# State space matrices turned inside a feed-forward layer's last step, and the mixer's closing units in split products

## The chip, the cores and the metric

The kernel runs on one core of a Trainium2 chip. The metric is device time in microseconds (us) for one execution of the whole program. TensorE is called PE in the profile, VectorE DVE, ScalarE ACT, GpSimd POOL and SyncE SP. "PEld" is PE's loading of weights, which overlaps with its matmuls.

## What is computed

256 tokens of width 1024 pass through two layers of a first block (a hybrid mixer, then a dense SwiGLU or eight experts) and two layers of a second block (SwiGLU, a mixer, SwiGLU). Two places matter here. The first is the end of the hybrid mixer, which runs once in each layer of the first block:

```
y_dn = o.reshape(B, S, DN_V) @ w_up_dn           # 1024 x 1024
y_sb = o_sb.reshape(B, S, SB_W) @ w_up_sb        #  512 x 1024
g_dn, g_sb = jnp.split(jax.nn.sigmoid(gates), N_BRANCH, axis=-1)
return (g_dn * y_dn + g_sb * y_sb) @ w_out       # 1024 x 1024
```

The second is the start of the second block's first mixer, a state space recurrence, which follows the third feed-forward layer (`ffn1_0`) of the program:

```
h = h + 0.5 * _swiglu(_rmsnorm(h, ffn1_norm[layer]), ffn1_w_in[layer], ffn1_w_out[layer])
u = _rmsnorm(h, mix_norm[layer])
bu_re = jnp.einsum('bsgh,gph->bsgp', ug, bb_re)  # ug: u in groups of 16 channels
bu_im = jnp.einsum('bsgh,gph->bsgp', ug, bb_im)
_, _, x_re, x_im = lax.associative_scan(combine, (la_re, la_im, bu_re, bu_im), axis=1)
```

## The kernel before

**Layout and order.** Activations lie with channels on the 128 partitions: 8 channel tiles of 256 tokens side by side. Each engine has its own list of instructions, written out by hand, and the lists meet only at semaphores; an instruction that waits holds up all that is behind it on its engine. Weights come in *units* of 128x2048 numbers (1 MB) through a ring of six buffers: SP loads unit n when unit n-6 is done (`unit_done` counts finished units). One unit holds 16 blocks of 128x128 and is multiplied with 256 tokens.

**Two ways to multiply a unit.** `cols_unit` (L419 to L431) multiplies plain f32 weights from the ring with f32 activations, 16 matmuls. `cols_split` (L488 to L497) takes weights and activations as two fp32r parts each, high and low, and makes three matmuls for each block (`product`, L483 to L486: high by high, high by low, low by high). For that, ACT copies a unit's high part to one of two places, `room[n % 2]` (`w_hi`, L2187 to L2191), and DVE subtracts it from the ring's unit, which gives the low part in `ring_low` (`w_low`, L1261 to L1266; its instruction has line L1234, as every `tt` of DVE has). `w_hi` of unit n waits until the units up to n-2 are done. The activations are split the same way in quarters of 128x512, counted by `h_high` and `h_low`. All feed-forward layers and the mixer's first projection use `cols_split`; `SPLITS` numbers the units in the order in which they are split, and `INPUTS` the split activations.

**The mixer's end** (`combine`, L709 to L732) has ten units, all in f32: `up` 0 to 3 (delta rule output by `w_up_dn`), `up` 4 and 5 (attention output by `w_up_sb`), `w_out` 0 to 3. Between `up` 0 and `up` 1 stands `stick` (L697), 16 small products of the attention, in banks 2 and 3 of PSUM; DVE copies these banks out (L1774, L1775, `stick_out`), and `up` 2 waits for that. DVE multiplies each `up` result with its gates as it comes, adds the two branches (`mixed`, by quarters), and adds the `w_out` results to the residual `X` (L1790). Unit `w_out` 0 is written out by itself (L728) since it takes the quarters of `mixed` as they come. Then come the sum of squares of the norm (`norm`, PE, L441), its logarithm and exponential (ACT, L2237 and L2238), and the normalising (DVE, L1253).

**The start of the recurrence.** The last unit of `ffn1_0` is the last step of `ffn_split` (L891): its results lie in banks 4 to 7, finished two tiles at a time (`bank_out`), and DVE adds each to `X` (L1875). Then PE sums squares for norm 6, DVE normalises (eight instructions, L1253), and only when all eight are done does PE turn the 16 blocks of the recurrence's input matrices (`BBX`, L1013), which DVE copies out of banks 0, 1, 4 and 5 (L1955) to `BBT`. After that PE makes the first products of channel block k = 0 (L1048) into banks 0 to 3, and DVE begins its loop over k: two multiplies out of PSUM, two sums, two scans (L1982, L1983), two multiplies. `BBX` itself was made by DVE beside the units of `ffn1_0`.

Of the kernel before, what the change touches and what calls it, by code (L numbers as in the profile page):

```python
# [22 lines left out]
P = 128  # L23
# [55 lines left out]
MIXER = dict(mixer_v=("a_abs", "gu", "cum_read", "kd_arg", "u_arg", "q_dec", "vnew0", "state", "vt_out", "vnew1", "stick_out"),  # L79
# [6 lines left out]
def program(nc, A):  # L86
    ctx = ExitStack()
    with ctx:
# [148 lines left out]

        def w_high(room, n):
            return room[n % 2]
# [4 lines left out]
        ROOM = ROOM_MIX = (SLOT["E"], SLOT["D"], SLOT["F"])  # L244
        ROOM_GLU = (11264, 13312, 23552)
# [3 lines left out]
        NORM_BANK = (7, 7, 0, 7, 7, 7, 0, 4, 0, None, 0, 7)  # L249
# [5 lines left out]
        for name, count in (("w_in0", 0), ("ffn", BLK1), ("w_in1", 0), ("ffn1_0", BLK2), ("ffn2_0", BLK2), ("ffn1_1", BLK2),  # L255
                            ("ffn2_1", BLK2)):
            SPLITS[name], SPLIT_BLOCKS[name] = splits, blocks_before
            splits += 3 * count if count else PROJECTIONS
            blocks_before += count
# [151 lines left out]
        def _(pe):  # L411
# [21 lines left out]
            def half(b, t):  # L433
                return bank[b][:, t * TOK:(t + 1) * TOK]

# [52 lines left out]
            def cols_split(n, dst, room, first=None):  # L488

                for t in range(2):  # L490
                    for k in range(KT):
                        if first is not None and t == 0 and k % 2 == 0:
                            pe.wait_ge(*at("h_low", k // 2 + 1, INPUTS[first]))
                        c = (k * 2 + t) * P
                        mm = product(dst(t), parts(w_high(room, n) + c, P), ring_low[n % RING][:, c:c + P],
                                     parts(h_high(room) + k * TOK, TOK), parts(HB + k * TOK, TOK), k == 0, k == KT - 1)
                mm.then_inc(sem("unit_done"), 1)  # L497
# [211 lines left out]
            def combine(l):  # L709
                n = UN[f"up{l}"]  # L710
                pe.wait_ge(*at("stick_arg", 2, l, 8))
                for u in range(4):
                    if u == 1:
                        stick(l)
                    if u == 2:
                        pe.wait_ge(*mixer("stick_out", l))
                    cols_unit(n + u, lambda t: half(u, t), src=BIG, src_off=OD,
                              quarter=None if u else lambda b: at("od", b, l, 4))
                for u in range(2):
                    cols_unit(n + 4 + u, lambda t: half(4 + 2 * u + t // 2, t % 2), kt=4, tiles=4, src=BIG, src_off=OSB)  # L720
# [10 lines left out]
                for u in range(1, 4):  # L731
                    cols_unit(n + u, lambda t: half(u, t), src=BIG, src_off=SLOT["D"])  # L732
# [158 lines left out]
            def ffn_split(name, blocks, base, room):  # L891
# [3 lines left out]
                def step(p, i=0):  # L895
# [13 lines left out]
                    else:  # L909
# [11 lines left out]
                        if p == 3 * blocks - 1:  # L921
                            if name == "ffn":
                                ada_later(MIX_UNITS, 12, bank[1], 0)

# [82 lines left out]
            norm(6, 0)  # L1007

            pe.wait_ge(*at("normed", 8, 6))
            pe.wait_ge(sem("bb"), 1)  # L1010
            for i in range(2):
                for k in range(KT):
                    mm = pe.transpose(bank[4 * i + k // 4][:, (k % 4) * P:(k % 4 + 1) * P], big(BBX + i * 1024 + k * P, P), ident)  # L1013
            mm.then_inc(sem("bt_ps"), 1)
# [26 lines left out]
            for k in range(KT + 2):  # L1041
                if k < KT:

                    if k:
                        pe.wait_ge(sem("bu_read"), k)
# [183 lines left out]
        def _(ve):  # L1229
# [356 lines left out]
            for l in range(LAYERS):  # L1586
# [186 lines left out]
                ve.wait_ge(*mixer("stick_ps", l))  # L1773
                ve.tensor_copy(big(OSB, 512), bank[2][:, :])  # L1774
                ve.tensor_copy(big(OSB + 512, 512), bank[3][:, :]).then_inc(mixer("stick_out", l)[0], 1)  # L1775

                n = UN[f"up{l}"]
                for b in range(4):
                    ve.wait_ge(sem("unit_done"), n + b + 1)
                    tt(big(SLOT["D"] + b * 512, 512), bank[b][:, :], big(GATES + b * 512, 512), ALU.mult)  # L1780
                for b in range(4):
                    if b % 2 == 0:
# [3 lines left out]
                        .then_inc(sem("mixed"), 1)  # L1786
                n = UN[f"w_out{l}"]
                for t in range(KT):
                    ve.wait_ge(sem("unit_done"), n + t // 2 + 1)
# [161 lines left out]
            norm_v(norms, ("mix_norm", 0), False)  # L1951
            norms += 1
            ve.wait_ge(sem("bt_ps"), 1)
            for b in range(4):
                ins = ve.tensor_copy(big(BBT + b * 512, 512), bank[(0, 1, 4, 5)[b]][:, :])  # L1955
# [3 lines left out]
            lk(ve.memset(view(SM, MAG, [[TOK, 4], [1, 1]]), 0.0))  # L1959
            for k in range(KT):  # L1960
# [220 lines left out]
        def _(se):  # L2181
# [5 lines left out]
            def w_hi(n, room, i=0):  # L2187

                se.wait_ge(sem(f"loaded{n % RING}"), i * 16 + 16 * (n // RING + 1))
                se.wait_ge(sem("unit_done"), i * RING + (n - 1))  # L2190
                act(parts(w_high(room, n), UNIT), ring[n % RING][:, :], ACT.Copy).then_inc(sem("w_high"), 1)  # L2191
# [163 lines left out]
            for l in range(LAYERS):  # L2355
# [484 lines left out]
```

## Time and profile before

| | us |
|---|---|
| median of 3 timed runs | 3281.03 |
| lowest, highest | 3277.46, 3284.76 |
| the profiled execution, device time | 3277.59 |
| its span in the trace | 3275.8 |
| granted PE clock, mean over the span | 0.971 |

Some 1.8 us of the profiled execution's time lie outside the span. All starts and durations below are of that one execution, in us from the start of its span. "The chain" is the chain of work that ended last, followed back from the last instruction; "issue" in it is time in which the engine waited for nothing that the profile shows.

### The profile page before, as it was taken

The page shows a single profiled execution, that of the slowest core. Times are in us where ns is not written, and L with a number is a line of the kernel's source. Part 1 is how long each engine was busy: PE and PEld are TensorE (multiplying, and loading weights), DVE is VectorE, ACT ScalarE, POOL GpSimd, SP SyncE. Part 2 cuts the span into 40 slices and gives each one's busy share as a digit, 9 for nine tenths or more (in the row PEclk, how much of TensorE's full clock was granted, in tenths as well). Part 3 has the DMA queues.
Part 4 walks back from the last instruction along what each step waited for, and adds up shares of the span by engine and source line. Part 5 has one row for each costly group of instructions (what it writes and reads, how often), then busy time and mean ns, then how long its engine had stood idle before and what let it go on. Part 6 is the DMA issues. An engine that isn't in the chain of part 4 may idle for free.

```text
span 3275.8 us, 48712 instructions
## 1 busy us (share of the span) xinstructions
PE 3129.9 (96%) x20334; PEld 2804.2 (86%) x20334; DVE 2290.1 (70%) x2552; ACT 1632.4 (50%) x1637; POOL 111.4 (3%) x118
## 2 busy tenths in 40 slices
PE   7999999999999999999999999899589999998999
PEld 7999899999898788888888888899259999995799
DVE  7975288838662888988988988597974435447344
ACT  3546144435461777777777777343114324435333
POOL 0004000000120000000000000000000000100000
PEclk8999999989999999999999999999689999998999
DMA  8640388735303699999999999354023543540253
GB/s 360 250 150 1 116 309 307 264 114 187 116 1 129 217 368 366 367 369 366 371 364 368 361 375 365 132 187 171 1 102 143 186 172 142 193 166 14 103 181 128
DMA packets 130019, 702.96 MB, mean 215 GB/s; under 512 B 11184, under 2 KB 15552, under 8 KB 74048
## 3 DMA queue, kind: packets, MB, share of 16 engines
q1 hardware_dynamic: 118816, 650.30, 53.8%
q0 software_dynamic: 6880, 48.24, 3.8%
q10 hardware_dynamic: 4160, 2.12, 0.3%
q8 instruction: 118, 1.93, 0.2%
q14 instruction: 45, 0.37, 0.0%
HBM read 698.50 MB, written 1.07 MB: 214 GB/s over the span
## 4 chain that ended last, share of the span: by engine, by line
PE 90%; DVE 6%; ACT 2%; issue 1%; POOL 1%; DMA 0%; SPq 0%; ACTq 0%; DVEq 0%
PE banks L484 23%; PE banks L485 23%; PE banks L486 23%; PE banks L428 7%; DVE big L1234 2%; PE banks L592 1%; PE banks L441 1%; PE banks L574 1%; PE banks L786 1%; DVE ring_low L1234 1%; PE banks L1063 1%; PE banks L480 1%; PE banks L580 1%; POOL tail L2628 1%; PE banks L807 1%
## 5 line engine op out<-in xcount | busy, mean ns | idle before, releaser
L1234 DVE TENSOR_TENSOR ring_low<-ring,parts 128x2048 fp32r<-128x2048 f32 x570 | 1297.6, 2287 | 375.9 <-ACT parts L2191 351.1
L484 PE MATMUL banks<-parts 128*128 128x256 f32 (+1 forms) x3712 | 1168.0, 315 | 20.9 <-DVE tail_parts L1234 17.5
L485 PE MATMUL banks<-tail_parts,parts 128*128 128x256 f32 x3744 | 1062.5, 284 | 0.0
L2191 ACT ACTIVATE parts<-ring 128x2048 fp32r<-128x2048 f32 x234 | 448.5, 1917 | 808.4 <-PE banks L486 708.6
L486 PE MATMUL banks<-parts,ring_low 128*128 128x256 f32 x2816 | 798.1, 283 | 0.0
L484 PEld LDWEIGHTS banks<-parts 128*128 128x128 f32 x3712 | 706.7, 190 | 61.8 <-issue 20.2
L2264 ACT ACTIVATE parts<-ring 128x2048 fp32r<-128x2048 f32 x336 | 644.8, 1919 | 211.7 <-DMA ring<-in_wall 207.9
L485 PEld LDWEIGHTS banks<-tail_parts,parts 128*128 128x128 f32 x3744 | 712.8, 190 | 1.9 <-issue 1.9
L486 PEld LDWEIGHTS banks<-parts,ring_low 128*128 128x128 f32 x2816 | 537.8, 191 | 0.0
L486 PE MATMUL banks<-parts,tail_parts 128*128 128x512 f32 x896 | 352.6, 394 | 0.0
L485 PE MATMUL banks<-ring_low,parts 128*128 128x512 f32 x896 | 352.5, 393 | 0.0
L484 PE MATMUL banks<-tail_parts,parts 128*128 128x256 f32 x928 | 263.0, 283 | 0.1
L486 PE MATMUL banks<-tail_parts,ring_low 128*128 128x256 f32 x928 | 262.6, 283 | 0.0
L486 PEld LDWEIGHTS banks<-parts,tail_parts 128*128 128x128 f32 x896 | 168.3, 188 | 40.7
L485 PEld LDWEIGHTS banks<-ring_low,parts 128*128 128x128 f32 x896 | 168.8, 188 | 33.9
L484 PE MATMUL banks<-parts,tail_parts 128*128 128x512 f32 x448 | 177.5, 396 | 1.0 <-DVE tail_parts L1234 1.0
L484 PEld LDWEIGHTS banks<-tail_parts,parts 128*128 128x128 f32 x928 | 177.1, 191 | 0.4 <-issue 0.4
L486 PEld LDWEIGHTS banks<-tail_parts,ring_low 128*128 128x128 f32 x928 | 176.8, 191 | 0.0
L485 PE MATMUL banks<-ring_low,tail_parts 128*128 128x512 f32 x448 | 176.3, 394 | 0.0
L486 PE MATMUL banks<-parts 128*128 128x512 f32 x448 | 176.3, 393 | 0.0
L428 PE MATMUL banks<-big,ring 128*128 128x256 f32 x768 | 167.4, 379 | 0.8 <-DVE big L2173 0.8
L428 PEld LDWEIGHTS banks<-big,ring 128*128 128x128 f32 x768 | 145.5, 190 | 21.2 <-DVE big L2173 1.2
(408 smaller groups left out, 3397.6 us busy)
## 6 DMA issues: line engine op xcount, KB each, us to landing
ring<-in_wall SPq DMA_DIRECT2D x616, 1024.0 KB, 6.5
big<-in_wall POOLq DMA_DIRECT2D x40, 1024.0 KB, 5.7
big<-in_w_k POOLq DMA_DIRECT2D x1, 2048.0 KB, 9.4
big<-in_w_v POOLq DMA_DIRECT2D x1, 2048.0 KB, 16.5
big<-bias_table ACTq DMA_DIRECT2D x2, 1024.0 KB, 7.8
constants<-in_con SPq DMA_DIRECT2D x1, 1249.5 KB, 9.4
x<-in_x SPq DMA_DIRECT2D x1, 1024.0 KB, 7.1
big<-big POOLq DMA_DIRECT2D x16, 64.0 KB, 5.1
```

What stands on the lines that cost most here:

```text
L428: mm = pe.matmul(dst(t), tile(n, k * tiles + t), src[:, src_off + k * width:src_off + (k + 1) * width], start=(k == 0), stop=(k == kt - 1))
L441: mm = pe.matmul(half(b, 0), ones, big(SQ0 + t * TOK, TOK), start=(t == 0), stop=(t == KT - 1))
L480: mm = pe.matmul(o[:, c:c + 1], ada_sum(first + n)[:, t * P:(t + 1) * P], ones[:, 0:1], start=True, stop=True)
L484: pe.matmul(o, high, in_high, start=start, stop=False, **kw)
L485: pe.matmul(o, high, in_low, start=False, stop=False, **kw)
L486: return pe.matmul(o, low, in_high, start=False, stop=stop, **kw)
L574: mm = pe.matmul(bank[q][:, c * P:(c + 1) * P], block(LTS, q, c), block(SLOT["E"], q, c), start=True, stop=True)
L580: mm = pe.transpose(bank[4 + q % 2][:, c * P:(c + 1) * P], block(SLOT["E"], q, c), ident)
L592: mm = pe.matmul(bank[6 + q % 2][:, c * P:(c + 1) * P], inverse_t, u, start=True, stop=True)
L1234: return ve.tensor_tensor(out, a, b, op)
L2191: act(parts(w_high(room, n), UNIT), ring[n % RING][:, :], ACT.Copy).then_inc(sem("w_high"), 1)
L2264: act(parts(slot_at(q), UNIT), ring[r][:, :], ACT.Copy).then_inc(sem("x_high"), 1)
```

## The change

In the mixer's end, `up` 1 to 5 and `w_out` 1 to 3 become split products; `up` 0 and `w_out` 0 stay in f32. ACT and DVE get the splitting of these eight weight units a layer and of three inputs (`OD`, the attention output, `mixed`), at the places in their lists that the diff shows. The copying of banks 2 and 3 by DVE becomes four half-bank copies by ACT and four subtractions by DVE. At the recurrence, the turning moves into the last step of `ffn1_0`, before its products; DVE copies the turned blocks right after its last addition to `X`; the norm's sum goes to bank 4; and PE's first products wait for their own channel block of the normalised input.

```diff
+        ROOM_UP, ROOM_OUT, SUM_LOW, OSB_HIGH = (0, CONV, SLOT["C"]), (0, CONV + 2048, SLOT["C"]), SLOT["B"], OSB + 1024
-        NORM_BANK = (7, 7, 0, 7, 7, 7, 0, 4, 0, None, 0, 7)
+        NORM_BANK = (7, 7, 0, 7, 7, 7, 4, 4, 0, None, 0, 7)
...
             def combine(l):
                 n = UN[f"up{l}"]
                 pe.wait_ge(*at("stick_arg", 2, l, 8))
-                for u in range(4):
-                    if u == 1:
-                        stick(l)
+                cols_unit(n, lambda t: half(0, t), src=BIG, src_off=OD, quarter=lambda b: at("od", b, l, 4))
+                stick(l)
+                for u in range(1, 4):
                     if u == 2:
-                        pe.wait_ge(*mixer("stick_out", l))
-                    cols_unit(n + u, lambda t: half(u, t), src=BIG, src_off=OD,
-                              quarter=None if u else lambda b: at("od", b, l, 4))
+                        pe.wait_ge(*at("h_low", 4, INPUTS[f"osb{l}"]))
+                    pe.wait_ge(sem("w_low"), SPLITS[f"od{l}"] + u)
+                    cols_split(n + u, lambda t: half(u, t), ROOM_UP, f"od{l}" if u == 1 else None, SUM_LOW)
                 for u in range(2):
-                    cols_unit(n + 4 + u, lambda t: half(4 + 2 * u + t // 2, t % 2), kt=4, tiles=4, src=BIG, src_off=OSB)
+                    pe.wait_ge(sem("w_low"), SPLITS[f"od{l}"] + 4 + u)
+                    for t in range(4):
+                        for k in range(4):
+                            c = (k * 4 + t) * P
+                            mm = product(half(4 + 2 * u + t // 2, t % 2), parts(w_high(ROOM_UP, n + 4 + u) + c, P),
+                                         ring_low[(n + 4 + u) % RING][:, c:c + P], parts(OSB_HIGH + k * TOK, TOK),
+                                         parts(OSB + k * TOK, TOK), k == 0, k == 3)
+                    mm.then_inc(sem("unit_done"), 1)
...
                 for u in range(1, 4):
-                    cols_unit(n + u, lambda t: half(u, t), src=BIG, src_off=SLOT["D"])
+                    pe.wait_ge(sem("w_low"), SPLITS[f"mixed{l}"] + u)
+                    cols_split(n + u, lambda t: half(u, t), ROOM_OUT, f"mixed{l}" if u == 1 else None, SUM_LOW)
```

PE, the last step of `ffn_split`, and then the start of the recurrence:

```diff
+                            if name == "ffn1_0":
+                                pe.wait_ge(sem("bb"), 1)
+                                for c in range(2 * KT):
+                                    turned_b = pe.transpose(bank[c // 4][:, (c % 4) * P:(c % 4 + 1) * P], big(BBX + c * P, P), ident)
+                                turned_b.then_inc(sem("bt_ps"), 1)
...
-            norm(6, 0)
-
-            pe.wait_ge(*at("normed", 8, 6))
-            pe.wait_ge(sem("bb"), 1)
-            for i in range(2):
-                for k in range(KT):
-                    mm = pe.transpose(bank[4 * i + k // 4][:, (k % 4) * P:(k % 4 + 1) * P], big(BBX + i * 1024 + k * P, P), ident)
-            mm.then_inc(sem("bt_ps"), 1)
+            norm(6, 4)
             pe.wait_ge(sem("bt"), 1)
...
+                    pe.wait_ge(*at("normed", k + 1, 6))
```

DVE, the mixer's end, behind the attention's arguments:

```diff
-                ve.wait_ge(*mixer("stick_ps", l))
-                ve.tensor_copy(big(OSB, 512), bank[2][:, :])
-                ve.tensor_copy(big(OSB + 512, 512), bank[3][:, :]).then_inc(mixer("stick_out", l)[0], 1)
+                def sum_low(name, source):
+                    for b in range(4):
+                        ve.wait_ge(*at("h_high", b + 1, INPUTS[name]))
+                        tt(parts(SUM_LOW + b * 512, 512), big(source + b * 512, 512),
+                           parts(h_high(ROOM_UP) + b * 512, 512).bitcast(F32), ALU.subtract).then_inc(sem("h_low"), 1)
...
+                sum_low(f"od{l}", OD)
+                w_low(n + 1, SPLITS[f"od{l}"] + 1, ROOM_UP)
+                for c in range(4):
+                    ve.wait_ge(*at("h_high", c // 2 * 2 + 2, INPUTS[f"osb{l}"]))
+                    tt(parts(OSB + c * TOK, TOK), half(2 + c // 2, c % 2), parts(OSB_HIGH + c * TOK, TOK).bitcast(F32), ALU.subtract)                        .then_inc(sem("h_low"), 1)
+                w_low(n + 2, SPLITS[f"od{l}"] + 2, ROOM_UP)
                 for b in range(4):
                     ve.wait_ge(sem("unit_done"), n + b + 1)
                     tt(big(SLOT["D"] + b * 512, 512), bank[b][:, :], big(GATES + b * 512, 512), ALU.mult)
+                    if b:
+                        w_low(n + 2 + b, SPLITS[f"od{l}"] + 2 + b, ROOM_UP)
+                w_low(n + 7, SPLITS[f"mixed{l}"] + 1, ROOM_OUT)
...
+                sum_low(f"mixed{l}", SLOT["D"])
                 n = UN[f"w_out{l}"]
                 for t in range(KT):
+                    if t in (0, 2):
+                        w_low(n + 2 + t // 2, SPLITS[f"mixed{l}"] + 2 + t // 2, ROOM_OUT)
```

DVE, the start of the recurrence:

```diff
             ffn2("ffn1_0", 0)
+            ve.wait_ge(sem("bt_ps"), 1)
+            for b in range(4):
+                ins = ve.tensor_copy(big(BBT + b * 512, 512), bank[b][:, :])
+            lk(ins)
+            ve.nop().then_inc(sem("bt"), 1)
+
+            lk(ve.memset(view(SM, MAG, [[TOK, 4], [1, 1]]), 0.0))
             norm_v(norms, ("mix_norm", 0), False)
             norms += 1
-            ve.wait_ge(sem("bt_ps"), 1)
-            for b in range(4):
-                ins = ve.tensor_copy(big(BBT + b * 512, 512), bank[(0, 1, 4, 5)[b]][:, :])
-            lk(ins)
-            ve.nop().then_inc(sem("bt"), 1)
-
-            lk(ve.memset(view(SM, MAG, [[TOK, 4], [1, 1]]), 0.0))
```

ACT, the mixer's end, behind the attention's exponentials (`w_hi` gets an argument `done`, 1 where nothing is said, and waits for `unit_done` to reach `n - done`):

```diff
+                def sum_high(b, source):
+                    act(parts(h_high(ROOM_UP) + b * 512, 512), big(source + b * 512, 512), ACT.Copy).then_inc(sem("h_high"), 1)
+                n = UN[f"up{l}"]
+                for b in range(4):
+                    se.wait_ge(*at("od", b + 1, l, 4))
+                    sum_high(b, OD)
+                w_hi(n + 1, ROOM_UP)
+                w_hi(n + 2, ROOM_UP)
+                se.wait_ge(*mixer("stick_ps", l))
+                for c in range(4):
+                    act(parts(OSB_HIGH + c * TOK, TOK), half(2 + c // 2, c % 2), ACT.Copy).then_inc(sem("h_high"), 1)
+                for u in range(3, 6):
+                    w_hi(n + u, ROOM_UP)
+                w_hi(n + 7, ROOM_OUT, done=2)
+                for b in range(4):
+                    se.wait_ge(*at("mixed", b + 1, l, 4))
+                    sum_high(b, SLOT["D"])
+                w_hi(n + 8, ROOM_OUT)
+                w_hi(n + 9, ROOM_OUT)
```

## Rows read from the trace of the kernel before

**Rows 1.** The page: busy time by engine, and the chain by engine.

```profile
PE 3129.9 (96%) x20334; PEld 2804.2 (86%) x20334; DVE 2290.1 (70%) x2552; ACT 1632.4 (50%) x1637; POOL 111.4 (3%) x118
PE 90%; DVE 6%; ACT 2%; issue 1%; POOL 1%; DMA 0%; SPq 0%; ACTq 0%; DVEq 0%
```

**Rows 2.** The chain at both mixers' ends: start us, us, what.

```profile
349.77 34.73 PE banks L428 x160
384.50 6.91 PE banks L728 x32
391.41 20.72 PE banks L428 x96
412.13 3.47 PE banks L441 x16
991.41 34.73 PE banks L428 x160
1033.05 20.72 PE banks L428 x96
```

**Rows 3.** Windows: one split unit, then five f32 units (clock and DMA share behind).

```profile
2276.43:2282.15 5.72, 5.72 (x49) 5.72 (x49) 2.08 (x3) 1.90 (x3) 0.00 (x0) 1.00 0.52 186
349.77:384.50 34.73, 34.73 (x162) 30.60 (x162) 6.63 (x10) 0.00 (x0) 0.00 (x0) 1.00 0.40 140
```

**Rows 4.** Timelines of ACT and DVE: splitting of a weight unit, of a quarter.

```profile
427.76 1.91 ACT L2191 ACTIVATE parts<-ring 128x2048 fp32r<-128x2048 f32 x1 [4.71 <-PE banks L486]
422.41 0.63 ACT L2250 ACTIVATE parts<-tail 128x512 fp32r<-128x512 f32 x1
429.70 2.29 DVE L1234 TENSOR_TENSOR ring_low<-ring,parts 128x2048 fp32r<-128x2048 f32 x1 [3.74 <-ACT parts L2191]
420.16 0.69 DVE L1234 TENSOR_TENSOR tail_parts<-tail,parts 128x512 fp32r<-128x512 f32 x1
```

**Rows 5.** Timelines of ACT, DVE and PE around the first f32 unit and stick.

```profile
340.44 1.77 ACT L2473 ACTIVATE big<-big 128x768 f32<-128x768 f32 x2 [1.03 <-DVE big L1234]
339.39 1.94 DVE L1234 TENSOR_TENSOR big<-big,banks 128x384 f32<-128x384 f32 x4
346.90 0.66 PE L704 MATMUL banks<-big,tail 128*64 128x256 f32 x4
2327.71 0.38 ACT L2511 ACTIVATE big<-banks 128x256 f32<-128x256 f32 x1 [0.17 <-PE banks L1063]
```

**Rows 6.** Timeline of DVE: gates and branch sums.

```profile
377.63 0.69 DVE L1234 TENSOR_TENSOR big<-banks,big 128x512 f32<-128x512 f32 x1 [6.21 <-PE banks L428]
378.97 0.68 DVE L1234 TENSOR_TENSOR big<-banks,big 128x512 f32<-128x512 f32 x1
```

**Rows 7.** The chain at the start of the recurrence.

```profile
2282.15 3.47 PE banks L441 x16
2286.60 3.26 DVE tail L1253 x8
2289.91 3.00 PE banks L1013 x16
2292.93 2.49 DVE big L1955 x4
2295.53 2.13 PE banks L1048 x16
2297.75 4.50 DVE big L1234 x2
```

**Rows 8.** Timeline of PE: four transposes, and what follows, in the delta rule.

```profile
260.55 0.60 PE L580 MATMUL banks<-constants,big 128*128 128x128 f32 x4
260.99 1.06 PE L574 MATMUL banks<-big,tail 128*128 128x128 f32 x8
```

**Rows 9.** Timeline of DVE: its last addition to X before norm 6.

```profile
2282.19 0.69 DVE L1875 SCALAR_TENSOR_TENSOR x<-banks,x 128x512 f32<-128x512 f32 x1 [0.74 <-PE banks L486]
```

**Rows 10.** Windows of 4 us in and behind the recurrence: granted clock third from the end.

```profile
2288.00:2292.00 4.00, 2.09 (x13) 2.10 (x14) 1.85 (x5) 0.00 (x0) 0.00 (x0) 0.83 0.00 0
2420.00:2424.00 4.00, 4.00 (x23) 4.00 (x22) 3.97 (x3) 0.00 (x0) 0.00 (x0) 0.55 0.02 4
```

More of the change, by code:

```diff
@@ L78 @@
 SUMMED = (0, 1, 2, 3, 4, 5, 6, 7, 8, 10, 11)
-MIXER = dict(mixer_v=("a_abs", "gu", "cum_read", "kd_arg", "u_arg", "q_dec", "vnew0", "state", "vt_out", "vnew1", "stick_out"),
+MIXER = dict(mixer_v=("a_abs", "gu", "cum_read", "kd_arg", "u_arg", "q_dec", "vnew0", "state", "vt_out", "vnew1", ),
              mixer_s=("beta_exp", "a_ln", "decay_exp", "u_exp", "w_neg"),
@@ L232, in parts, with half @@
             return PARTS[:, off:off + width]
+        def half(b, t):
+            return bank[b][:, t * TOK:(t + 1) * TOK]
         def w_high(room, n):
@@ L254, in program @@
         splits = blocks_before = 0
-        for name, count in (("w_in0", 0), ("ffn", BLK1), ("w_in1", 0), ("ffn1_0", BLK2), ("ffn2_0", BLK2), ("ffn1_1", BLK2),
-                            ("ffn2_1", BLK2)):
+        for name, count, blocks in (("w_in0", PROJECTIONS, 0), ("od0", 5, 0), ("osb0", 0, 0), ("mixed0", 3, 0), ("ffn", 3 * BLK1, BLK1),
+                                    ("w_in1", PROJECTIONS, 0), ("od1", 5, 0), ("osb1", 0, 0), ("mixed1", 3, 0),
+                                    ("ffn1_0", 3 * BLK2, BLK2), ("ffn2_0", 3 * BLK2, BLK2), ("ffn1_1", 3 * BLK2, BLK2),
+                                    ("ffn2_1", 3 * BLK2, BLK2)):
             SPLITS[name], SPLIT_BLOCKS[name] = splits, blocks_before
-            splits += 3 * count if count else PROJECTIONS
-            blocks_before += count
+            splits += count
+            blocks_before += blocks
         INPUTS = {name: i for i, name in enumerate(SPLITS)}
@@ L431, in cols_unit @@
                 mm.then_inc(sem("unit_done"), 1)
-            def half(b, t):
-                return bank[b][:, t * TOK:(t + 1) * TOK]
             def norm(i, b):
@@ L486, in product, with cols_split @@
                 return pe.matmul(o, low, in_high, start=False, stop=stop, **kw)
-            def cols_split(n, dst, room, first=None):
+            def cols_split(n, dst, room, first=None, low=HB):
                 for t in range(2):
@@ L495, in cols_split @@
                         mm = product(dst(t), parts(w_high(room, n) + c, P), ring_low[n % RING][:, c:c + P],
-                                     parts(h_high(room) + k * TOK, TOK), parts(HB + k * TOK, TOK), k == 0, k == KT - 1)
+                                     parts(h_high(room) + k * TOK, TOK), parts(low + k * TOK, TOK), k == 0, k == KT - 1)
                 mm.then_inc(sem("unit_done"), 1)
@@ L1950, in _ @@
             ffn2("ffn1_0", 0)
-            norm_v(norms, ("mix_norm", 0), False)
-            norms += 1
             ve.wait_ge(sem("bt_ps"), 1)
             for b in range(4):
-                ins = ve.tensor_copy(big(BBT + b * 512, 512), bank[(0, 1, 4, 5)[b]][:, :])
+                ins = ve.tensor_copy(big(BBT + b * 512, 512), bank[b][:, :])
             lk(ins)
@@ L1959, in _ @@
             lk(ve.memset(view(SM, MAG, [[TOK, 4], [1, 1]]), 0.0))
+            norm_v(norms, ("mix_norm", 0), False)
+            norms += 1
             for k in range(KT):
@@ L2185, in lk, with w_hi @@
                 link(se, "scalar_step", ins)
-            def w_hi(n, room, i=0):
+            def w_hi(n, room, i=0, done=1):
                 se.wait_ge(sem(f"loaded{n % RING}"), i * 16 + 16 * (n // RING + 1))
-                se.wait_ge(sem("unit_done"), i * RING + (n - 1))
+                se.wait_ge(sem("unit_done"), i * RING + (n - done))
                 act(parts(w_high(room, n), UNIT), ring[n % RING][:, :], ACT.Copy).then_inc(sem("w_high"), 1)
```

## The prediction

> **What bounds the kernel now.** I read the page's busy times and its chain first, then the chain in order of time around the two places that change, then the timelines of ACT and DVE there, and last the windows for the granted clock. The page says that PE is busy 96% of the span and carries 90% of the chain, DVE 6% [rows 1]. So time is won where PE's own work shrinks, or where PE and DVE hand the chain to each other for nothing. Both places show one of these. At the mixer's end the chain is PE alone, without a gap: `up` 1 to 5 run in 34.73 us, `w_out` 0 in 6.91, `w_out` 1 to 3 in 20.72, and norm 1 follows at 412.13; layer 1 repeats it [rows 2]. An f32 unit thus costs 6.91 us at the full clock (the window says 1.00) [rows 3]. In those 34.73 us DVE works 6.63 us and ACT not at all [rows 3]: there is room for splitting. At the recurrence the chain changes hands six times: norm sum, normalising by DVE, turning by PE, copies by DVE, the first products by PE, and DVE's loop from 2297.75 on [rows 7].
>
> **The mixer's end, PE.** A split unit in the feed-forward layer before norm 6 takes 5.72 us at clock 1.00, with its 48 matmuls of 128x256 and without idle time [rows 3]. That row is for the same matmul shapes that the eight units of a layer get. `up` 4 and 5 have another order (4 tiles by 4 blocks) but the same 16 blocks. So `up` 1 to 5 go from 34.73 to 28.60 (6.13 less), `w_out` 1 to 3 from 20.72 to 17.16 (3.56 less): 9.69 us a layer if PE never waits.
>
> The Trainium skill, FP8 and Floating Point Precision, section TensorE Precision Notes, says that a true FP32 product takes four passes through the array. Three products in place of four passes would make a unit 5.18 us (three quarters of 6.91), and the gain 13.8 us a layer in place of 9.69. The row of the split unit disagrees: 5.72, and the sum goes by the row.
>
> **Does the splitting keep up?** One weight unit costs ACT 1.91 us, then DVE 2.29; a quarter of activations 0.63 and 0.69 [rows 4]. I walk through layer 0.
>
> *Start.* ACT's exponentials end at 342.2 and DVE's arguments at 341.3 [rows 5]. ACT copies four quarters (about 0.54 apiece back to back) to 344.4 and unit `up` 1 to 346.3; DVE follows with its quarters to 345.1 and the unit from 346.3 to 348.6. `stick` begins at 346.90 [rows 5] and gives way to `up` 1 at 349.77 [rows 2]. So `up` 1 starts on time, with 1.1 us to spare; `up` 0 and `stick` are the work that hides this. Without them the 1.91 + 2.29 us would stand in the open.
>
> *Attention output.* ACT's copy for `up` 2 waits for `up` 0 (about 347.0) and ends at 348.9. Behind it stand the four half-bank copies, which start when `stick` is done; 0.38 us for 256 columns out of PSUM [rows 5], about 0.3 apiece in a run, so to 351.1. DVE subtracts to 351.8 and only then makes the low part of `up` 2, to 354.1. `up` 1 ends at 349.8 + 5.7 = 355.5: 1.4 us to spare. The two DVE copies that this replaces lay in the same place, beside `up` 1.
>
> *Steady state.* A unit's high part can start when the unit two before it is done, so the pair has one unit's duration, 5.72 us. It needs 1.91 + 2.29 and a hop between engines, 4.3 us. DVE's gate multiply of 0.69 [rows 6] falls in the 1.91 of ACT. That leaves 1.4 us at each of `up` 3 to 5. By this walk `up` 4 ends at 372.7 and `up` 5 at 378.4.
>
> *Into `w_out`.* Here the order in DVE's list costs something. The low part of `w_out` 1 stands ahead of the sums with the second branch. ACT starts its high part when `up` 4 is done (`done=2`), 372.7 to 374.6; DVE makes the low part until 376.9. Only then come the first two pairs of gate multiply and sum, 1.34 us a pair [rows 6], so `mixed` 1 at 378.3, `mixed` 2 at 379.7, 3 at 381.0 and 4 at 382.4. `w_out` 0 starts at 378.4, uses the first quarter for 0.86 us (4 of 32 instructions of 6.91 us) and stands 0.4 us for the second; the others are there before their turn, since both tiles of the first half come first. I take 0.5 us. In the kernel before, the first two quarters were long there when `up` 5 ended. `w_out` 0 ends at about 385.8. What is late next: ACT's quarters of `mixed` at 383.1, DVE's at 384.9, so `w_out` 1 has 0.9 us to spare. `w_out` 2 and 3 are split as in the steady state (each DVE part before two X updates of 0.88 together, which wait for units long done). PE then ends about 9.2 us earlier than 412.13. The norm behind it is as before, for it hangs on the last X update; ACT's list is empty there.
>
> Bounds of this part: 9.69 a layer with no stall. The other end is a stall as long as the smallest margin lets through: if each of seven hand-overs (all but the first) took 1.9 us longer than I sum, 0.5 us of it would show at each, 3.5 us a layer. I take 9.2, twice 18.4.
>
> SP's loads are triggered by `unit_done` and come at 5.7 in place of 6.9 us: the DMA share was 0.40 there and 0.52 in a stretch at the new pace [rows 3], so they stay hidden. POOL's loads wait for the X updates, as before.
>
> **The recurrence.** Before, DVE's loop starts 2297.75 - 2282.15 = 15.60 us after the last product of `ffn1_0` [rows 7]. Removed from that stretch are the turning (3.00), the copies (2.49), and the first products (2.13), with their hops [rows 7]. The first products of k = 0 now need only the first of DVE's eight normalising instructions: PE starts 0.5 us after 2286.60 and needs 2.13, so it ends at 2289.2, under DVE's 3.26, which end at 2289.86 [rows 7]. DVE then goes straight on at 2289.90, 7.85 us earlier. The copies need cover: the last addition to X ends at 2282.88 [rows 9], four copies end at 2285.4, the two links and the memset at about 2285.8, and the reciprocal root that DVE waits for comes at 2286.60: 0.8 us to spare. Without it, 2.49 would be back. ACT's first scalar row waits for the copies too, and is wanted only by the scan, some 7 us into the loop.
>
> Added is the turning in front of the last step's products. PE has no idle time there (5.72 busy of 5.72) [rows 3], so it costs all it lasts. 16 transposes cost 3.00 us where they were, but the clock was 0.83 and falling there [rows 7, 10]. At full clock four of them pass in 0.44 us (260.55 to 260.99) [rows 8], so sixteen in 1.76. `ffn1_0` runs at clock 1.00, so I take 1.76; 3.00 is the other end. Their four banks were read before the wait on the last `g_low`, which PE does anyway. Gain: 7.85 - 1.76 = 6.1 us (4.8 at the other end). It is kept: everything behind starts from DVE's loop.
>
> **The sum.** 18.4 + 6.1 = 24.5 us. Against the profiled execution's own 3277.59 (1.8 outside the span) that is 3253.1. The runs' median lies 3.4 above it, which gives 3256.5. I take 3255, between the two. 0.2%, what a measurement of this kernel can tell from no change, is 6.6 us.
>
> **Rivals.**
> 1. *Late feed.* The hand-overs cost more than I sum and 0.5 us shows at seven places a layer: 3255 + 7 = 3262. For it: three engines in turn, margins of 0.9 to 1.4 us. Against: the feed-forward layers feed their units by the same two instructions and run without idle time [rows 3]. Chance 0.08.
> 2. *The feed sets the pace at about the old one*, 6.9 us a unit: nothing is won at the mixer. It needs 2.6 us more in each round than the rows give. Then only the 6.1 us of the recurrence stay: 3273, no measurable change. Chance 0.04.
> 3. *The feed is serial, and the kernel slower.* Place: the room of a unit's high part. If it came free only when the unit just before is done, each of the 16 units would cost 5.72 + 1.91 + 2.29 = 9.92 in place of 6.91, 48 us in all less the 6.1: 3321. A serial unit costs 3.0 and a good one gives 1.2, so with the recurrence's gain it decides from about six serial units of the sixteen. Against it: two rooms alternate, as in the feed-forward layers. Chance 0.03.
> 4. *The recurrence gives 2 us or less*, because the copies delay the normalising, or because the PE waits inside DVE's loop grow by what was won at its start: 3259. Chance 0.04.
> 5. *A split block costs three quarters of an f32 one.* PE would need 5.18 us a unit, 8.6 us less than my sum over 16 units: 3246. [...] The trace does not agree (5.72). Chance 0.03.
>
> My forecast has the remaining 0.78. Its own spread comes from the clock. It drops when PE pauses, and even in a busy stretch (0.55 at 2420) [rows 10]. A shifted program meets these drops at other points, each worth a microsecond or two, and the timed runs spread over 7.3 us. Rivals 1 and 4 lie inside 3246 to 3264, rival 5 at its lower edge, 2 and 3 outside. Faster: 0.78 + 0.08 + 0.04 + 0.03 = 0.93; same 0.04; slower 0.03.
>
> **What the changed profile would show.** The eight units a layer take 28.6 and 17.2 us in the chain, lines 484 to 486 in place of 428. PE idles about 0.4 us within `w_out` 0, released by DVE, and nowhere else in the mixer's end. The turning takes 1.8 us before the last step of `ffn1_0`. DVE's first loop multiply follows the eight normalising instructions at once. I would be wrong if PE idles before `up` 1 or at each split unit with DVE as the releaser, if the 16 transposes take 3 us, or if DVE's normalising waits for its own copies.

## The result

The changed kernel takes 3257.91 us (median of 4 runs, 3253.88 to 3259.99), the kernel before 3279.53 us in the runs timed with it (4 runs, 3277.46 to 3284.76). The ratio is 0.993 with a 95% interval of 0.9913 to 0.9947: 21.6 us less by the medians, 17.4 to 28.5 by the interval. The forecast was 3255.0, inside 3246 to 3264, and "faster by over 0.2%" (6.6 us). The profiled execution took 3257.01 us with a span of 3255.2, 20.6 less than the span of before.

The chain of the changed kernel at the mixer's end of layer 0, in order of time (L434 is `cols_unit`, L738 is `w_out` 0, L444 the norm sum, L2218 and L1244 are ACT's and DVE's splitting):

```profile
340.23 6.91 PE banks L434 x32
373.11 1.93 ACT parts L2218
375.06 2.29 DVE ring_low L1244
377.98 1.30 DVE big L1244 x2
380.06 6.31 PE banks L738 x28
403.51 3.47 PE banks L444 x16
```

These answer to [rows 2], and to one more row of the chain before, the start of its `up` 0:

```profile
340.06 6.91 PE banks L428 x32
```

From the start of `up` 0 to the norm sum it is now 63.28 us; before it was 72.07 (412.13 less 340.06). The split matmuls between these rows are too short and too many to be listed. The window over the whole stretch, DVE's list where the chain leaves PE, and PE's list at the same place:

```profile
340.23:403.51 63.28, 63.05 (x482) 60.16 (x481) 36.14 (x41) 27.61 (x27) 0.00 (x0) 1.00 0.42 150
```

```profile
369.34 2.29 DVE L1244 TENSOR_TENSOR ring_low<-ring,parts 128x2048 fp32r<-128x2048 f32 x1 [1.31 <-ACT parts L2218]
375.06 2.29 DVE L1244 TENSOR_TENSOR ring_low<-ring,parts 128x2048 fp32r<-128x2048 f32 x1 [3.42 <-ACT parts L2218]
377.27 0.68 DVE L1244 TENSOR_TENSOR big<-banks,big 128x512 f32<-128x512 f32 x1
377.98 0.69 DVE L1244 TENSOR_TENSOR big<-big 128x512 f32<-128x512 f32 x1
378.59 0.68 DVE L1244 TENSOR_TENSOR big<-banks,big 128x512 f32<-128x512 f32 x1
379.31 0.69 DVE L1244 TENSOR_TENSOR big<-big 128x512 f32<-128x512 f32 x1
```

```profile
378.44 0.28 PE L489 MATMUL banks<-parts,ring_low 128*128 128x256 f32 x1
378.82 7.54 PE L738 MATMUL banks<-big,ring 128*128 128x256 f32 x32
```

PE is busy 63.05 of 63.28 us at clock 1.00, and DVE's low parts start 5.72 us apart (369.34 and 375.06), the pace of the split unit: the feed keeps up. DVE waits 3.42 us for ACT before it makes the low part of `w_out` 1 (375.06), and its gate multiplies stand behind that. The first sum is ready at 378.67, the second at 380.00. The last product of `up` 5 starts at 378.44 and such products follow each other every 0.12 us (48 in 5.72), so the first sum comes 0.1 us too late, and `w_out` 0 starts at 378.82. It then has the matmuls of one quarter before it needs the second sum: the chain comes back to L738 with 28 of 32 instructions left, at 380.06, and the unit's 32 matmuls take 7.54 us from first start to last end.

The chain at the recurrence, which answers to [rows 7] (L938 is the turning, L1263 the normalising, L1244 DVE's first loop multiplies):

```profile
2263.26 1.75 PE banks L938 x16
2270.72 3.47 PE banks L444 x16
2275.25 3.26 DVE tail L1263 x8
2278.50 4.41 DVE big L1244 x2
```

The turning costs 1.75 us in the last step of `ffn1_0`, and DVE's loop follows the normalising without a gap, 7.78 us after the last product in place of 15.60. The copies lie in DVE's list directly behind its last addition, and DVE still waits 1.15 us for ACT's root after them:

```profile
2271.37 2.47 DVE L1980 COPY big<-banks 128x512 f32<-128x512 f32 x4
2274.03 0.06 DVE L1984 MEMSET small<- 128x4 f32 x1 [0.19 <-DVE big L1980]
2275.25 3.26 DVE L1263 SCALAR_TENSOR_TENSOR tail<-x,parameters,inverse_rms 128x256 f32<-128x256 f32 x8 [1.15 <-ACT inverse_rms L2265]
```

**Where 3 us went.** The stretches that the change touches are shorter by 8.79, 8.78 and 7.82 us, and `ffn1_0` pays 1.75. That makes 23.64, not 20.6. The chains show where time came back: from norm 1 to norm 2, code that the diff leaves alone, it was 259.72 us before and is now 262.21; from norm 3 to the gathering of tokens 17.61 and now 19.25. These two make 4.1 us; all the other stretches that the change leaves alone together are 1.1 us shorter (behind the glu units 2.4 less, DVE's loop 1.0 more). Windows from the first feed-forward product to norm 2 and from norm 3 to the gathering, with PE's busy time and matmul records and the granted clock third from the end, first before, then changed:

```profile
419.53:671.85 252.32, 251.71 (x2065) 0.98 0.75 283
1053.77:1071.38 17.61, 12.90 (x71) 0.81 0.16 61
```

```profile
410.91:665.72 254.81, 254.46 (x2065) 0.97 0.74 281
1038.89:1058.14 19.25, 14.54 (x70) 0.73 0.17 55
```

The extra time is PE's busy time, 2.75 and 1.64 us more for the same matmuls at a lower granted clock, and no longer wait. Windows of 2 us at the start of the first feed-forward layer show the difference (the granted clock stands third from the end). First the kernel before, then the changed one:

```profile
419.00:421.00 2.00, 1.19 (x7) 0.92 (x7) 2.00 (x5) 1.94 (x6) 0.00 (x0) 0.79 0.96 389
421.00:423.00 2.00, 2.00 (x9) 1.89 (x10) 1.31 (x3) 1.97 (x4) 0.00 (x0) 0.50 1.04 434
423.00:425.00 2.00, 2.00 (x14) 1.85 (x14) 1.92 (x2) 0.04 (x1) 0.00 (x0) 0.85 1.00 422
```

```profile
409.00:411.00 2.00, 0.09 (x1) 0.12 (x1) 1.55 (x4) 1.94 (x5) 0.00 (x0) 0.80 0.97 365
411.00:413.00 2.00, 2.00 (x9) 1.96 (x10) 2.00 (x6) 1.97 (x5) 0.00 (x0) 0.50 1.02 426
413.00:415.00 2.00, 2.00 (x11) 1.90 (x9) 1.23 (x3) 1.40 (x3) 0.00 (x0) 0.50 1.01 426
415.00:417.00 2.00, 2.00 (x10) 1.90 (x10) 2.00 (x2) 0.00 (x0) 0.00 (x0) 0.50 1.02 430
417.00:419.00 2.00, 2.00 (x19) 2.00 (x18) 0.35 (x1) 0.00 (x0) 0.00 (x0) 1.00 0.73 307
```

In both, PE idles some 4 us for the norm, the clock falls to 1.2 GHz (0.50) at about the time when PE starts again, and the first products run at that level. Before, it was back at 2.4 GHz after some 3.5 us; now it stays low for about 7. The experiments had to say whether the change does that. (The clock fell ahead of norm 2 as well, in both: it was 0.50 from 664 to 668 before and from 656 to 660 now.)

### The profile page after: what moved, and what is told of

Same layout as the page of the kernel before. It is cut to its first block, busy times and chain, and to the rows that moved or that the text cites. A ratio compares the mean times of both kernels' runs of the same rounds, so it can differ in the third digit from the quotient of the medians.

```text
span 3255.2 us, 49327 instructions
## 1 busy us (share of the span) xinstructions
PE 3113.2 (96%) x20590; PEld 2801.0 (86%) x20590; DVE 2335.6 (72%) x2588; ACT 1675.0 (51%) x1677; POOL 111.3 (3%) x118
## 4 chain that ended last, share of the span: by engine, by line
PE 89%; DVE 7%; ACT 2%; issue 1%; POOL 1%; DMA 1%; SPq 0%; ACTq 0%; DVEq 0%
PE banks L487 24%; PE banks L488 23%; PE banks L489 23%; PE banks L434 4%; DVE big L1244 2%; PE banks L595 1%; PE banks L444 1%; PE banks L577 1%; DVE ring_low L1244 1%; PE banks L797 1%; PE banks L483 1%; PE banks L583 1%; POOL tail L2677 1%; DVE tail L1244 1%; DMA ring<-in_wall 1%
## 5 line engine op out<-in xcount | busy, mean ns | idle before, releaser
L1244 DVE TENSOR_TENSOR ring_low<-ring,parts 128x2048 fp32r<-128x2048 f32 x586 | 1334.3, 2287 | 411.5 <-ACT parts L2218 379.7
L487 PE MATMUL banks<-parts 128*128 128x256 f32 (+1 forms) x3968 | 1240.3, 313 | 21.5 <-DVE tail_parts L1244 18.1
L2218 ACT ACTIVATE parts<-ring 128x2048 fp32r<-128x2048 f32 x250 | 479.2, 1917 | 797.7 <-PE banks L489 752.7
L489 PE MATMUL banks<-parts,ring_low 128*128 128x256 f32 x3072 | 869.8, 283 | 0.0
L487 PEld LDWEIGHTS banks<-parts 128*128 128x128 f32 x3968 | 754.7, 190 | 63.3 <-issue 20.5
L2291 ACT ACTIVATE parts<-ring 128x2048 fp32r<-128x2048 f32 x336 | 644.9, 1920 | 208.1 <-DMA ring<-in_wall 202.2
L489 PEld LDWEIGHTS banks<-parts,ring_low 128*128 128x128 f32 x3072 | 585.8, 191 | 0.0
L1244 DVE TENSOR_TENSOR big<-big 128x512 f32<-128x512 f32 (+6 forms) x141 | 124.8, 891 | 29.1 <-ACT big L2575 20.1
L1244 DVE TENSOR_TENSOR tail<-tail,banks 128x256 f32<-128x256 f32 (+1 forms) x170 | 86.0, 506 | 55.0 <-PE banks L489 49.1
```

What stands on the lines that cost most here:

```text
L487: pe.matmul(o, high, in_high, start=start, stop=False, **kw)
L489: return pe.matmul(o, low, in_high, start=False, stop=stop, **kw)
L1244: return ve.tensor_tensor(out, a, b, op)
L2291: act(parts(slot_at(q), UNIT), ring[r][:, :], ACT.Copy).then_inc(sem("x_high"), 1)
```

## The experiments

Stretches are read off each kernel's chain, in us of its one profiled execution; all kernels are listed together behind the experiments. Times of kernels with one run say nothing to 0.1%, so the stretches carry those verdicts.

### Each part alone, and both kernels once more

`mixer_only` is the changed kernel with the recurrence as before, `turn_only` the kernel before with the recurrence as changed:

```diff
 # mixer_only, against the changed kernel (PE; the turning in ffn1_0 and the waits per block are gone, DVE has the old order too)
-            norm(6, 4)
+            norm(6, 0)
+
+            pe.wait_ge(*at("normed", 8, 6))
+            pe.wait_ge(sem("bb"), 1)
+            for i in range(2):
+                for k in range(KT):
+                    mm = pe.transpose(bank[4 * i + k // 4][:, (k % 4) * P:(k % 4 + 1) * P], big(BBX + i * 1024 + k * P, P), ident)
+            mm.then_inc(sem("bt_ps"), 1)
...
```

> The change without its recurrence part: the mixer's end in split products, the turning, copies and waits at the recurrence as before. Theory: each of the two mixer ends is about 8.8 us shorter than before (72.07 to 63.3 us from up 0 to norm 1, as in the changed kernel's trace), 17.6 us in all, and the recurrence's start stays at 15.6 us between the last product of ffn1_0 and DVE's loop. About 3262 us. If instead the two parts only work together, or the recurrence part carries most of the gain, this kernel lies within 7 us of before.

Measured: 3264.75 us (6 runs) against 3279.48 before, ratio 0.9951 (0.9937 to 0.9964). Both mixer ends take 63.3 us, and the recurrence's start 15.62, as expected. The median is 2.8 above the expectation; its trace has the 262.10 and 19.25 us of the changed kernel's in the two stretches named above.

> The recurrence part alone, the mixer's end as before. Theory: 15.60 us become 7.8 and the turning adds 1.75 to ffn1_0, so 6.1 us less: about 3273 to 3274 us, at the edge of what can be told from no change. Rival: DVE's loop meets PE waits that grow by what was won, and the stretch from DVE's first loop multiply to the glu units (139.95 us before) grows by 4 us or more.

Measured: 3275.06 us (12 runs), ratio 0.9983 (0.9975 to 0.9992), so 2.6 to 8.2 us less by the interval. The start takes 7.78 us, the turning 1.75. The rival has a number on its side: DVE's loop to the glu units took 141.01, 1.06 more than the 139.95 of before. That is not the 4 us that it asked for, and the loop ranges from 137.76 to 141.02 over all kernels here, whatever they do at its start.

> The kernel before once more, for a second trace. Theory of the missing 3 us: the granted clock falls and rises at points that are not tied to the program, so the same stretches (the first units of the feed-forward layer, norm 2, the router, the recurrence) cost 1 to 3 us more or less from one execution to the next, while stretches at clock 1.00 repeat within 0.1 us. Rival: the change itself makes these stretches longer; then this trace repeats that of before in each of them within 0.3 us.

> The changed kernel once more, for a second trace. Theory: the mixer's ends repeat at 63.3 us and the recurrence's start at 7.8 us within 0.1 us, but the stretch from the first feed-forward product to norm 2 (254.81 us, 252.32 before), the stretch from norm 3 to the gathering (19.25, 17.61 before) and DVE's loop with its tail (140.98, 139.95 before) come out different from the first trace by 1 us or more in at least one of them. Rival, the change made them longer: they repeat.

Measured: 3278.94 and 3258.57 us, one run each. The two traces of before agree within 0.04 us from norm 1 to norm 2 (259.72, 259.76) and to the gathering (17.61, 17.63), as the rival says, and differ by 1.8 in the experts (986.05, 987.84) and in the units behind the glu (219.62, 217.80). The two traces of the changed kernel differ where the theory asks for it: 262.21 and 261.34 from norm 1 to norm 2, 19.25 and 17.61 to the gathering, 309.88 and 311.44 from norm 2 to the mixer of layer 1. `turn_only` helps further: up to norm 2 it runs the instructions of the kernel before, starts `up` 0 within 0.8 us of it, and takes 261.94 from norm 1 to norm 2, with the clock at 0.50 for some 7 us behind norm 1 (0.50 in the windows from 418 to 424). So 262 us there need no split mixer, and `both_better` below takes 258.35 with one, its clock back at 1.00 after some 3.5 us. For the 1.6 us behind norm 3 the table of all stretches says something else.

### What each step of the recurrence part is worth

`all_eight` brings back the wait for all normalising instructions, `copies_late` the old place of the copies:

```diff
 # all_eight (PE)
             norm(6, 4)
+            pe.wait_ge(*at("normed", 8, 6))
             pe.wait_ge(sem("bt"), 1)
 # copies_late (DVE)
             ffn2("ffn1_0", 0)
+            norm_v(norms, ("mix_norm", 0), False)
+            norms += 1
             ve.wait_ge(sem("bt_ps"), 1)
             for b in range(4):
                 ins = ve.tensor_copy(big(BBT + b * 512, 512), bank[b][:, :])
...
-            norm_v(norms, ("mix_norm", 0), False)
-            norms += 1
```

> The changed kernel, but PE's first recurrence products wait for all eight normalising instructions, as before. Theory: they no longer hide under DVE's normalising and stand in the open, 2.1 us, so from the last product of ffn1_0 to DVE's loop 9.9 us in place of 7.78. If the per-block waits were worth nothing, 7.8.

> The changed kernel, but DVE copies the turned blocks after its normalising, as before. Theory: 2.5 us of copies, their links, and the first products of 2.1 us behind them stand in the open: from the last product of ffn1_0 to DVE's loop about 12.6 us in place of 7.78, which is 15.6 less the 3.0 of the turning. If the copies did not matter, 7.8; if the first products could hide all the same, 10.4.

The chain of `all_eight`, then that of `copies_late`:

```profile
2273.03 3.27 DVE tail L1264 x8
2276.34 2.13 PE banks L1059 x16
2278.50 4.50 DVE big L1245 x2
```

```profile
2276.40 3.25 DVE tail L1263 x8
2279.65 2.41 DVE big L1982 x4
2282.16 2.13 PE banks L1058 x16
2284.39 4.50 DVE big L1244 x2
```

From the last product to DVE's loop they take 9.99 and 12.44 us (expected 9.9 and 12.6); the kernels took 3258.45 and 3261.81 us, one run each. The 7.82 us thus come apart as 3.2 for the turning that left the stretch, 2.4 for the copies and 2.2 for the first products. The early copies give their part also with the wait for all eight (9.99); the waits per block give theirs only once the copies are early, since the first products stand behind the copies otherwise.

### The split units with a serial feed

The prediction's rival on the slower side, made true for seven of the eight units of a layer:

```diff
-                w_hi(n + 1, ROOM_UP)
-                w_hi(n + 2, ROOM_UP)
+                w_hi(n + 1, ROOM_UP, done=0)
+                w_hi(n + 2, ROOM_UP, done=0)
...
-                    w_hi(n + u, ROOM_UP)
+                    w_hi(n + u, ROOM_UP, done=0)
...
-                w_hi(n + 8, ROOM_OUT)
-                w_hi(n + 9, ROOM_OUT)
+                w_hi(n + 8, ROOM_OUT, done=0)
+                w_hi(n + 9, ROOM_OUT, done=0)
```

> The changed kernel, but the high part of each split unit in the mixer's end except w_out 1 waits until the unit just before is done. Theory (the two rooms are what makes the split units pay): ACT's 1.92 and DVE's 2.29 stand in the open at up 3 to 5, w_out 2 and 3 (4.3 us each), some 5.8 at up 2, where the attention output is copied behind the high part, and 1.5 at up 1, which starts behind stick anyway: 63.28 us become about 92 per layer, the kernel about 3315 us, slower than before. Rival: ACT and DVE hide their part anyway in each other's work; then 63.3 stays.

Measured: 3339.81 us (2 runs) against 3277.75, ratio 1.0187 (1.0158 to 1.0217). A mixer end takes 106.6 us in layer 0 (norm sum at 446.09, `up` 0 at 339.46) and 106.2 in layer 1. The sign and the waits are as expected, the size is not: 43 us more than 63.3, where 29 were forecast. ACT's and DVE's lists and two windows of `serial_feed` show a wait, that for `up` 3 in layer 0, and what it brings with it:

```profile
371.36 1.91 ACT L2218 ACTIVATE parts<-ring 128x2048 fp32r<-128x2048 f32 x1 [11.53 <-PE banks L489]
373.31 2.29 DVE L1244 TENSOR_TENSOR ring_low<-ring,parts 128x2048 fp32r<-128x2048 f32 x1 [9.17 <-ACT parts L2218]
```

```profile
372.00:376.00 4.00, 0.35 (x1) 0.35 (x2) 2.69 (x2) 1.27 (x1) 0.00 (x0) 0.87 0.80 262
376.00:380.00 4.00, 4.00 (x20) 4.00 (x20) 0.20 (x1) 0.00 (x0) 0.00 (x0) 0.50 0.00 0
```

PE idles 4.3 us while the two engines split a unit, the granted clock falls to 0.50, and the unit behind it runs at half rate at first: 20 matmuls in 4 us, 0.2 us each, where 0.12 is the pace at 1.00. `up` 2 took 8.2 us (363.08 to 371.28 in the chain) in place of 5.72. The missing 14 us a layer are of this kind: in the chain of layer 0 `up` 2 to 5 and `w_out` 2 and 3 took 7.5 to 8.8 us each from their first product to what follows them, 14.5 in all above six times 5.72. The Trainium skill, TensorE: Matmul & The Clock Gate, section HAM oscillation — how this bites in real kernels, describes this pattern, stretches of work with waits between that each begin at the low clock; here the trace agrees (0.50 at 376 to 380), but for `up` 1, which ran at 1.00 and took 6.07.

### The stall in w_out 0

```diff
-                w_low(n + 7, SPLITS[f"mixed{l}"] + 1, ROOM_OUT)
                 for b in range(4):
...
                     tt(big(SLOT["D"] + b * 512, 512), big(SLOT["D"] + b * 512, 512), big(SLOT["E"] + b * 512, 512), ALU.add)\
                         .then_inc(sem("mixed"), 1)
+                    if b == 1:
+                        w_low(n + 7, SPLITS[f"mixed{l}"] + 1, ROOM_OUT)
```

> The changed kernel, but in DVE's list the low part of w_out 1 stands behind the first two pairs of gate multiply and sum, not ahead of them. Theory: the first two quarters of mixed are there when up 5 ends, w_out 0 starts at once and runs its 6.91 us, and a mixer end takes 62.4 us in place of 63.28 (9.69 less than the 72.07 of before). Rival: the stall is that of PE changing from split to f32 products, or of the third and fourth quarter; then 63.3 stays or the stall moves into the middle of w_out 0.

Measured: 3255.81 us, one run. Both mixer ends take 62.55 us, 0.73 less than 63.28 (0.9 was expected), and the detour over ACT and DVE is gone from the chain of `sums_first`. Its chain, and PE's list at the same place:

```profile
378.08 6.91 PE banks L738 x32
402.13 3.47 PE banks L444 x16
```

```profile
377.80 0.28 PE L489 MATMUL banks<-parts,ring_low 128*128 128x256 f32 x1
377.91 7.07 PE L738 MATMUL banks<-big,ring 128*128 128x256 f32 x32
```

Only the order in DVE's list was changed, so the stall is DVE's order. It had two parts: `w_out` 0 now starts 0.11 us after the last product of `up` 5 started, where it was 0.38, and takes 7.07 us, where it was 7.54. 72.07 less 62.55 is 9.52; the 9.69 of eight units at 5.72 is reached but for 0.17.

### The turning where PE idles, and both improvements

```diff
-            norm(6, 4)
-            pe.wait_ge(sem("bt"), 1)
+            norm(6, 0)
+            pe.wait_ge(sem("bb"), 1)
+            for b in (0, 2, 1, 3):
+                for c in range(4):
+                    mm = pe.transpose(bank[4 + b][:, c * P:(c + 1) * P], big(BBX + (4 * b + c) * P, P), ident)
+                mm.then_inc(sem("bt_ps"), 1)
+            pe.wait_ge(sem("bt"), 2)
...
+                    if k == 4:
+                        pe.wait_ge(sem("bt"), 4)
...
 # ACT, behind the norm's exponential; DVE's copies are gone
+            for i, b in enumerate((0, 2, 1, 3)):
+                se.wait_ge(sem("bt_ps"), i + 1)
+                act(big(BBT + b * 512, 512), bank[4 + b][:, :], ACT.Copy).then_inc(sem("bt"), 1)
```

> The changed kernel, but PE turns the 16 blocks right behind the sum of norm 6, where it idles, into banks 4 to 7, and ACT copies them out, two banks before the first products and two later; the norm's sum is in bank 0 again. Theory: the 1.75 us before the last step of ffn1_0 are gone, and from the last product to DVE's loop it stays 7.8 us, so 1.75 us less in all. Rival: ACT's copies delay the first products beyond DVE's normalising, and the stretch grows by up to 1 us.

Measured: 3256.66 us, one run. The timelines of PE and ACT in `turn_in_gap`:

```profile
2273.69 1.03 PE L444 MATMUL banks<-tail,constants 128*128 128x256 f32 x4
2274.55 1.91 PE L1023 MATMUL banks<-constants,big 128*128 128x128 f32 x16
2276.70 1.15 PE L1061 MATMUL banks<-tail,big 32*128 32x256 f32 x16 [0.24 <-ACT big L2555]
```

```profile
2275.58 2.04 ACT L2555 ACTIVATE big<-banks 128x512 f32<-128x512 f32 x4
```

The turning follows the norm sum, ACT copies from 2275.58 on, the first products wait 0.24 us and end at 2277.85, before DVE's normalising does (2278.96 in the chain). The stretch is 7.71 us, and there is no turning in `ffn1_0`.

> Both improvements at once: the turning in PE's idle time behind norm 6 with copies by ACT, and DVE's sums ahead of the low part of w_out 1. Theory: 1.75 and twice 0.85 us, 3.4 us less than the changed kernel: about 3254 to 3255 us, about 25 below before. This is less than the spread of the runs, so the medians may hide it; the stretches in the trace decide.

Measured: 3250.57 us (5 runs, 3249.47 to 3255.50) against 3279.29 before, ratio 0.9916 (0.9902 to 0.9929). The stretches are 62.55, 62.55 and 7.70. It has the lowest median of all versions. That is 4 us under the expectation; of its span's 6.4 us under the changed kernel's, 3.9 lie between norm 1 and norm 2 (258.35 for 262.21), which neither edit touches. The interval overlaps that of the changed kernel, so the gain over it, 3.3 us by the stretches and the turning, is shown by these and not by the times.

### All stretches

Each column is a stretch from one mark in the chain to the next; the marks are `up` 0 of layer 0, norms 1 and 2, `up` 0 of layer 1, norm 3, the gathering, the scattering, the last product of `ffn1_0`, DVE's loop, the glu units. What lies ahead of the first mark, behind the last, and between the scattering and the last product is left out. "Mixer" columns and "start" are those that the change touches.

```
               mixer 0  norm1-2  -up0(1)  mixer 1  -gather  experts  start   loop
before           72.07   259.72   309.85    72.07    17.61   986.05  15.60  139.95
before_again     72.07   259.76   309.87    72.07    17.63   987.84  15.32  139.66
turn_only        72.07   261.94   309.91    72.07    17.62   988.48   7.78  141.01
mixer_only       63.27   262.10   309.89    63.28    19.25   985.85  15.62  139.91
after            63.28   262.21   309.88    63.29    19.25   986.63   7.78  140.98
after_again      63.28   261.34   311.44    63.28    17.61   987.06   7.78  139.66
all_eight        63.29   261.35   311.47    63.28    17.62   986.18   9.99  139.50
copies_late      63.30   262.08   309.89    63.29    19.25   986.24  12.44  140.24
sums_first       62.55   262.30   309.90    62.55    18.62   987.75   7.78  141.02
turn_in_gap      63.29   262.11   309.91    63.28    19.25   987.80   7.71  137.76
both_better      62.55   258.35   311.47    62.55    17.63   988.74   7.70  140.07
```

The touched stretches repeat within 0.03 us among kernels that share their code (the start of before within 0.3). The others range over 1.6 to 4 us. Taken one by one they do not go with an edit: 19.25 and 17.61 both appear with the same changed kernel, and so do 309.88 and 311.44. But the sum of these two columns, "-up0(1)" and "-gather", does. It is 327.5 us in the three executions with the mixer's end as before, and in `serial_feed` (309.91 and 17.62), and 328.5 to 329.2 in all eight with a mixer's end of 62.55 to 63.30 us. So in these twelve traces 1.0 to 1.7 of the 3 us go with the shorter mixer's ends, though the diff leaves these stretches alone. That a shifted program meets the clock's drops elsewhere, as the prediction has it, fits this; no run tested it.

## Why the prediction was right

- **A split unit costs 5.72 us.** Held: a mixer end whose stall is gone is 9.52 us shorter, against 9.69 from that row. The three quarters of rival 5 would have given 13.8; for these shapes the ratio is 5.72 to 6.91, 0.83.
- **The feed keeps up.** Held: PE busy 63.05 of 63.28 us, and DVE's low parts 5.72 us apart. `serial_feed` shows that the two rooms carry this. Rivals 1 to 3 fell.
- **The stall in `w_out` 0.** Right cause, too small: 0.5 us a layer was taken, and 9.69 less 8.79 is 0.90. Of this `sums_first` brings back 0.73. Within `w_out` 0, where the prediction had it, PE lost 0.47 (7.54 against 7.07), as forecast. What the prediction lacked is 0.26 us ahead of `w_out` 0: it had the first sum at 378.3, just before `up` 5 ends at 378.4, and the sum came at 378.67, 0.1 us after that end, since the low part of `w_out` 1 ran from 375.06 and not from 374.6. What remains, 0.17, is open.
- **The recurrence.** 7.85 forecast, 7.82 measured; the turning 1.76 and 1.75, at full clock as read from the delta rule's four transposes and not at the 3.00 of its old place, where the granted clock over these 3.00 us was 0.63. The copies had 1.15 us to spare where 0.8 was forecast. Rival 4 fell.
- **The sum.** 24.5 forecast; the touched stretches give 23.64; the span shows 20.6 and the medians 21.6. The 0.86 between the first two is the mixer's (18.4 forecast, 17.57 measured). The 3 us between the second and the span are the net of all that the change leaves alone; its two largest increases are PE at the lower clock. The prediction had put this into its range ("a shifted program meets these drops at other points") and not into its number.

The choice of 3255, between the sum from the profiled execution and that from the median of three runs, was a guess that came out well: with the fourth run the median of before is 3279.53, and less 24.5 that is 3255.03. So the miss of 2.9 us is the sum's, 0.9 at the mixer and 2.0 in code that was not changed. The code that no edit touches took 1.6 us more in the second execution than in the first, of the kernel before as of the changed one, so a miss of 2 us there neither speaks for the sum nor against it.

## What to carry to other kernels

Turning an f32 product into three split ones pays the difference of two rows per unit, here 1.19 us of 6.91, and only while other engines make the parts a unit ahead; with a serial feed the same products were slower than f32, since waits cost twice, once as time and once as clock. In a list of instructions written by hand, put what the bound engine waits for next ahead of what it needs a unit later: this was the only stall of more than 0.2 us that the change left in the mixer's end. And judge an edit of some microseconds by the stretches that it touches, because the rest of the program moves by as much without it, and in part with it.

## What the runs showed of the hardware

The same instructions from norm 1 to norm 2 took from 258.35 to 262.30 us in eleven executions, norm 3 to the gathering 17.6, 18.62 or 19.25. In the traces that were opened window by window, the difference is how long the granted clock stayed at 1.2 GHz after PE had idled for the norm: some 3.5 us in `before` and `both_better`, about 7 in `after` and `turn_only`. What decides between them in a given execution was not settled: both occur with the old mixer's end and with the new one. I had expected a microsecond or two at each such point, and the stretch from norm 1 to norm 2, which has two of them, ranged over four.
